# Second block: the gates' added row in one TensorE pass over 128 rows, and the convolution's columns turned inside the first gate

## The reference, cut to what matters

```python
h = rmsnorm_2(x, g_mix[l])
proj = jnp.einsum('bsd,dc->bsc', h, w_in[l])
q_a, k_a, v_a, q_i, k_i, w_i, conv_in, q_m, gate_logits = jnp.split(proj, split_points, axis=-1)
...
o_a = dsa_attention(q_a, k_a, v_a, q_i, k_i, w_i, topk)
o_b = conformer_conv(conv_in, conv_w[l], conv_b[l], ln_g[l], ln_b[l])   # u = a * sigmoid(gte), then 31 taps
o_m = memory_attention(q_m, mem, g_mem[l], w_mem_kv[l], g_qm[l], g_km[l])
gates = jax.nn.sigmoid((gate_logits + b_gate[l]).astype(jnp.float32)).astype(x.dtype)
gates = gates.reshape(B, S, N_BRANCHES, D)
merged = (gates[:, :, 0] * (o_a @ w_br_a[l]) + gates[:, :, 1] * (o_b @ w_br_b[l])
          + gates[:, :, 2] * (o_m @ w_br_m[l]))
```

## Time and profile before

| what | value |
|---|---|
| device time, three runs | 1715.82, 1716.11, 1717.97 us; median 1716.11 us |
| the profiled execution: its own time | 1714.42 us |
| its span, first to last instruction | 1712.6 us |
| TensorE / VectorE / ScalarE busy | 96% / 71% / 51% of the span |
| mean granted TensorE clock | 0.976 |
| L1786, the added row: matmul records | 24, at 587 ns in the median and up to 1214 ns |
| where they lie | 1123.3 to 1249 us of the span |

### The profile page before, as it was taken

One profiled execution on the slowest core, in us unless ns is written; L12 is line 12 of the kernel. 1 busy time (PEld: TensorE's weight loads), 2 busy tenths in 40 slices (PEclk: granted clock), 3 DMA queues, 4 the chain that ended last, 5 costly groups with the idle time before them and its releaser, 6 DMA issues.

```text
span 1712.6 us, 19789 instructions
## 1 busy us (share of the span) xinstructions
PE 1640.2 (96%) x7803; PEld 1299.2 (76%) x7803; DVE 1221.9 (71%) x1721; ACT 869.3 (51%) x1244; POOL 55.4 (3%) x87
## 2 busy tenths in 40 slices
PE   6999999999999999999999999999989999999998
PEld 2888877888868887668788888766768888787776
DVE  3989987989876855535655555685487578888986
ACT  3545454444454444355544444544355357776874
POOL 1010100000000000000000001000010000000000
PEclk9999999999999999999999999998599999999999
DMA  9998857988868754422655544442033338998993
GB/s 349 375 348 294 315 164 249 321 285 299 287 222 267 247 187 161 162 98 85 230 181 192 190 137 127 157 154 95 25 101 92 99 139 315 349 317 306 347 336 127
DMA packets 199603, 373.77 MB, mean 218 GB/s; under 512 B 8928, under 2 KB 102550, under 8 KB 199504
## 3 DMA queue, kind: packets, MB, share of 16 engines
q1 hardware_dynamic: 184080, 316.28, 54.2%
q0 software_dynamic: 15024, 55.07, 9.2%
q10 hardware_dynamic: 400, 1.10, 0.2%
HBM read 371.37 MB, written 1.05 MB: 217 GB/s over the span
## 4 chain that ended last, share of the span: by engine, by line
PE 86%; DVE 7%; ACT 5%; issue 1%; DMA 1%; SPq 0%; DVEq 0%; ACTq 0%
PE banks L520 23%; PE banks L522 23%; PE banks L521 23%; PE banks L747 2%; PE banks L1298 2%; PE banks L1325 1%; ACT full L719 1%; PE banks L1777 1%; DVE ul L464 1%; PE banks L672 1%; PE banks L889 1%; ACT uh L453 1%; PE banks L2249 1%; PE banks L2294 1%; PE banks L1312 1%; PE banks L1786 1%
## 5 line engine op out<-in xcount | busy, mean ns | idle before, releaser
L464 DVE TENSOR_TENSOR ul<-raw,uh 128x1024 fp32r<-128x1024 f32 (+2 forms) x548 | 659.2, 1210 | 216.9 <-ACT uh L453 208.3
L453 ACT ACTIVATE uh<-raw 128x1024 fp32r<-128x1024 f32 (+2 forms) x548 | 571.3, 1050 | 466.3 <-PE banks L522 457.6
L520 PE MATMUL banks<-uh,hh 128*128 128x512 f32 (+2 forms) x1280 | 522.2, 408 | 8.4 <-DVE hl L784 5.4
L522 PE MATMUL banks<-uh,hl 128*128 128x512 f32 (+2 forms) x1280 | 499.9, 391 | 0.0
L521 PE MATMUL banks<-ul,hh 128*128 128x512 f32 (+2 forms) x1280 | 499.0, 390 | 0.0
L520 PEld LDWEIGHTS banks<-uh,hh 128*128 128x128 f32 x1280 | 243.5, 190 | 72.5 <-issue 12.7
L521 PEld LDWEIGHTS banks<-ul,hh 128*128 128x128 f32 x1280 | 243.7, 190 | 53.1 <-issue 7.7
L522 PEld LDWEIGHTS banks<-uh,hl 128*128 128x128 f32 x1280 | 243.2, 190 | 50.6
L520 PE MATMUL banks<-uh,bh 128*128 128x512 f32 x528 | 209.8, 397 | 9.4 <-DVE bl L943 4.2
L522 PE MATMUL banks<-uh,bl 128*128 128x512 f32 x528 | 205.9, 390 | 0.0
L521 PE MATMUL banks<-ul,bh 128*128 128x512 f32 x528 | 205.6, 389 | 0.0
(11 more groups left out here) (311 smaller groups left out, 1400.3 us busy)
## 6 DMA issues: line engine op xcount, KB each, us to landing
raw<-in_ffn_w_in SPq DMA_DIRECT2D x176, 512.0 KB, 5.3
raw<-in_w_up SPq DMA_DIRECT2D x64, 1024.0 KB, 5.6
arena<-in_ada_w POOLq DMA_DIRECT2D x46, 1024.0 KB, 7.8
raw<-in_ffn_w_out SPq DMA_DIRECT2D x44, 1024.0 KB, 6.9
raw<-in_w_down SPq DMA_DIRECT2D x32, 1024.0 KB, 5.3
raw<-in_ada_w SPq DMA_DIRECT2D x26, 1024.0 KB, 6.7
raw<-in_w_in SPq DMA_DIRECT2D x22, 1024.0 KB, 5.0
raw<-in_w_mem_kv SPq DMA_DIRECT2D x4, 1024.0 KB, 5.9
```

The costliest lines, as they stand in the source:

```text
L453: act.e.activation(uh[r][:, 0:w], raw[m % NRAW][:, h * w:(h + 1) * w], AF.Copy).then_inc(act_done, ta.put("hi", u))
L464: dve.e.tensor_tensor(ul[r][:, 0:w], raw[m % NRAW][:, h * w:(h + 1) * w], uh[r][:, 0:w].bitcast(F32), ALU.subtract).then_inc(dve_done, tv. ...
L520: pe.e.matmul(o, a, wh, start=s0, stop=False)
L522: mm = pe.e.matmul(o, b, wh, start=False, stop=s1)
```

## The change

1. A new tile `gb` of 128 rows x 520 fp32r columns. Columns 0 to 511 hold the high parts of the six added rows in rows 0 to 5, their low parts in rows 32 to 37, and zeros elsewhere. Columns 512 to 517 hold the selection: column j has a one in rows j and 32 + j. `gate_rows_dve` fills it with five VectorE instructions and stands in VectorE's program between the norm's parts and the projections; it waits for both loads of `b_gate`.
2. `b_gate` is loaded twice on POOL's queue, to `adab[0:6]` and `adab[32:38]`.
3. A gate's added row is one fp32r matmul over all 128 rows for each bank (`gsel` x `gbias`), in place of the float32 one over 6 rows. It waits for `gate_rows_dve` in place of the load.
4. `conv_turn`, with its two counterparts on ScalarE and VectorE, moves from the middle of projection 3 to the middle of gate (0,0).
5. To make room, the second probability buffer is `adab`, and the arena, `cc` and `st` shrink.

```diff
@@ memory
-ARENA = 11332
+ARENA = 10816
-        cc = sb("cc", [P, 48])
+        cc = sb("cc", [P, 46])
-        st = sb("st", [P, 280])
+        st = sb("st", [P, 278])
+        gb = sb("gb", [P, 520], F32R)
-        pr6 = [wide_bufs[2], A(512)]
+        pr6 = [wide_bufs[2], adab[:, :]]
@@ gates
+        gsel, gbias = gb[:, 512:518], gb[:, 0:512]
+
+        def gate_rows_dve(dve):
+            low = gb[32:38, 0:512]
+            dve.wait_ge(loaded("b_gate"), 32)
+            dve.e.memset(gb[:, 0:518].bitcast(F32), 0.0).then_inc(dve_done, tv.put())
+            dve.own()
+            dve.e.tensor_tensor(gsel[0:38, :], ident[0:38, 0:6], ident[0:38, 32:38], ALU.add).then_inc(
+                dve_done, tv.put())
+            dve.e.tensor_copy(gbias[0:6, :], adab[0:6, :]).then_inc(dve_done, tv.put())
+            dve.e.tensor_copy(low, adab[32:38, :]).then_inc(dve_done, tv.put())
+            dve.own()
+            dve.e.tensor_tensor(gbias[32:38, :], adab[32:38, :], low.bitcast(F32), ALU.subtract).then_inc(
+                dve_done, tv.put("gb"))
+
-        def gates_pe(pe, g, c):
+        def gates_pe(pe, g, c, mid=None):
             j = 2 * g + c
-            pe.wait_ge(loaded("b_gate"), 16)
+            pe.wait_ge(dve_done, tv("gb"))
             for b in PAIRS[0]:
                 pe.take(b)
-                pe.e.matmul(PB[b], ident[0:6, j:j + 1].to_broadcast([6, P]), adab[0:6, :], start=True, stop=False)
-            linear(pe, ("gt",), KD, lh, ll, parts_ready(pe, "mix"), [[b] for b in PAIRS[0]], first=False,
+                pe.e.matmul(PB[b], gsel[:, j:j + 1].to_broadcast([P, P]), gbias, start=True, stop=False)
+            linear(pe, ("gt",), KD, lh, ll, parts_ready(pe, "mix"), [[b] for b in PAIRS[0]], first=False, mid=mid,
                    done=("gate", g, c))
...
@@ the three programs (TensorE's shown; ScalarE's and VectorE's likewise)
                 linear(pe, ("pj",), KD, lh, ll, parts_ready(pe, "mix"), [[b] for b in banks],
-                       mid=conv_turn if n == 3 else None, done=("pj", n))
+                       done=("pj", n))
...
-                    gates_pe(pe, g, c)
+                    gates_pe(pe, g, c, conv_turn if (g, c) == (0, 0) else None)
...
             scaled_dve(dve, "mix", KD, hh, hl, lambda k: col("g_mix_2", k), lambda k: 0.0)
+            gate_rows_dve(dve)
             dve.e.memset(uT[:, :, 0:30], 0.0).then_inc(dve_done, tv.put("u0"))
@@ POOL's loads
-            load("b_gate", adab[0:6, :], I["b_gate_2"].rearrange("a (j n) -> (a j) n", n=512))
+            for r in (0, 32):
+                load("b_gate", adab[r:r + 6, :], I["b_gate_2"].rearrange("a (j n) -> (a j) n", n=512))
```

More of the change, by code:

```diff
@@ L1790, in gates_pe, with gates_act @@
                 pe.frees(b, act_done, ta, "gate", g, c, t)
-        def gates_act(act, g, c):
-            units_act(act, ("gt",), KD)
+        def gates_act(act, g, c, mid=None):
+            units_act(act, ("gt",), KD, mid=mid)
             act.wait_ge(pe_done, tp("gate", g, c))
@@ L1908, in mix_act @@
             for n in range(len(PROJ)):
-                units_act(act, ("pj",), KD, mid=conv_turned if n == 3 else None)
+                units_act(act, ("pj",), KD)
                 act.wait_ge(pe_done, tp("pj", n))
@@ L1941, in mix_act @@
                 for c in range(2):
-                    gates_act(act, g, c)
+                    gates_act(act, g, c, conv_turned if (g, c) == (0, 0) else None)
             act.later.flush("qa")
@@ L1986, in mix_dve @@
             for n in range(len(PROJ)):
-                units_dve(dve, ("pj",), KD, mid=conv_weights if n == 3 else None)
+                units_dve(dve, ("pj",), KD)
                 if n == 1:
@@ L2002, in mix_dve @@
                     dve.later.add(heads_dve(dve, QA, lambda: taps_dve(dve, taps, 2)), "qa")
-            for _ in range(4):
-                units_dve(dve, ("gt",), KD)
+            for n in range(4):
+                units_dve(dve, ("gt",), KD, mid=conv_weights if n == 0 else None)
             dve.later.flush("qa")
```

## The result

The changed kernel's median was 1698.63 us in four runs (1697.13 to 1702.14) against 1715.96 for the kernel before; the ratio is 0.9899, with a 95% interval of 0.9881 to 0.9918. That is 17.3 us, where 13.6 were forecast; 1702.5 was predicted, 1698.5 to 1709 was the range. Single runs of both kernels scatter. I take 16.3 us as the gain to be explained; its 95% interval from these runs is 14.6 to 18.0.

What follows compares the result with a forecast made beforehand. TensorE, busy 96% of the span, was taken to bound the kernel. Row 9.65 plus clock 4.6 minus slower rise 0.7 gave 13.6 us, so 1716.11 became 1702.5 us; range 1698.5 to 1709.

Steps and rivals of the forecast that it cites:

- The added row: At six gate starts, one fp32r matmul per bank replaces the float32 one over 6 rows: 9.65 us gained.
- the 2.8 us set aside for it: Possible cost at the gates' added rows if a broadcast fp32r column's weight load took twice the matmul's 0.23 us, unhidden.
- The clock: After gates (2,0) and (2,1), both clock falls disappear as the light stretch ahead of the linear shortens: 4.6 us gained.
- larger gain: Whole kernel: more gained than forecast if the executions behind the median lose more falls than the profiled one; chance 0.03.
- The rise at gate (1,0): Behind the heads' flush, 0 to 2.7 us more at half speed before the clock rises: loss taken as 0.7 us.
- The turn: 1.38 us of TensorE work turning the columns moves from projection 3 to gate (0,0): net zero.
- Gate rows and second load: Ahead of the projections, five VectorE instructions (2.3 us, under 6.8 us of cover) and one more load: cost 0.
- VectorE late next: At the first head, VectorE's rotation of q would end 1.2 us ahead of TensorE's need: barely enough.
- Rival 1: In the gates, the clock falls stay, since only idle TensorE gaps cause them: 1707.1 us; chance 0.16.
- rival 3: At the added row, fp32r over a broadcast column runs like float32; no gain, falls stay: 1716.1 us; chance 0.05.
- rival 2: At the heads and keys' norm, VectorE's chain can't come earlier and takes TensorE's place: about 1710.6 us; chance 0.08.
- rival 4: Slower: clock falls at five gate starts and at the turn, 3.0 us each, 18 in all: 1720.5 us; chance 0.03.

Runs made afterwards that it cites:

- e5: Changed kernel, but the row is one plain float32 matmul per bank over all 128 rows, 122 of them zeros; 1708.72 us, ratio 0.9941 to the kernel before.
- e7: Changed kernel, but each bank gets four fp32r matmuls over all 128 rows in place of one; 1711.38 us, ratio 0.9958 to the kernel before.
- e6: Changed kernel, but each bank gets four fp32r matmuls over 6 rows in place of one over 128; 1716.02 us, ratio 0.9998 to the kernel before.
- e2: Kernel before with only the turn moved into gate (0,0), float32 row over 6 rows kept; 1717.18 us, ratio 0.9999 to the kernel before.
- e8: Changed kernel unaltered, measured again beside the kernel before in five rounds; 1701.61 us, ratio 0.9903.
- e11: Changed kernel unaltered, measured again as partner of other variants; 1700.67 us, ratio 0.9905 to the kernel before.
- e1: Changed kernel, but the turn of the columns stays in projection 3; median 1700.81 us, ratio 0.9905 to the kernel before.
- e3: Changed kernel, but gates (0,0), (2,0) and (1,1) use the other pair of banks; 1697.06 us, ratio 0.9886 to the kernel before.

## Why the prediction was right, and where its sizes were off

- **The added row, 9.65 us.** Its working has two errors that nearly cancel in the profile. The linear's first matmul comes 0.30 us later than I put it, since I left the second bank's weight load of 0.18 out of the sum. But before, the linear's first matmul took 0.43 us behind the row, at full clock, and now it takes 0.24 (L521 at 1138.09). Counted to the second matmul, gate (0,1) went from 2.41 us (1137.08 to 1139.49, by the earlier trace rows and that 0.43) to 1.23: 1.18 gained, forecast 1.27. Gate (1,0) gained 3.1, from 1229.66 to the second full matmul at 1234.09 before, against 1221.31 to 1222.59 now; 2.84 was forecast. Over many runs the row's time is worth somewhat less: the changed kernel against e5 gives 7.1 us in the means (about 2.3 to 11.9), and with the 1.2 of the first full matmuls, which e5 doesn't pay any more, 8.3. The weight load of a broadcast fp32r column, which I had no row for, takes 0.185 us in the median, and the 2.8 us set aside for it did not come.
- **The clock, 4.6 us.** The cause was right, rows at work, and e5 to e7 show it. The Trainium skill (TensorE: Matmul & The Clock Gate, "HAM oscillation") names only gaps in which TensorE is idle; here e6 lost the clock with TensorE as busy as in e7. The size was the term that failed: I took the falls of one execution for the kernel's, 1.6 + 2.7 + 0.3. The kernel before against e5 gives 9.2 us in the mean, 8.0 without the first full matmuls. The profile of e2, whose row is that of the kernel before, has four falls in the gates instead of two (its clock is below 1.00 in all three stretches shown above) and a span of 1719.9 us; the profiled one of before was among the quickest of its kind. This is the "larger gain" to which I gave 0.03. The prediction counted the idle 0.65 us ahead of the row into the light work, too; it stands unchanged in the changed kernel (0.69), without a fall, and whether it matters beside a row over 6 rows no run shows.
- **The rise at gate (1,0), loss 0.7.** The sign was wrong, by the very mechanism of the term before it: a row over 128 rows lets the clock rise earlier. The full matmuls began at 1222.17, and one cost 0.24 at 1223.87, 1.7 us later, against 3.2 before, some 0.7 us gained. Counted from the row's start the rise comes after 2.5 us here, 3.5 in e8 and 3.6 in e11, against 6.6 and 8.5 for the float32 row over 6 rows. This gain is part of the 8.0.
- **The turn, zero.** Shown by e1 and e2. VectorE's copy ran at 1134.14 with no wait ahead of it, and ScalarE's in its idle time.
- **Gate rows and second load, zero.** 2.2 us under a cover of 6.8.
- **VectorE late next, 1.2 us to spare.** 1.1 in the trace, and e3 used it up.
- **Sum.** 8.3 + 8.0 = 16.3 measured by parts, row and clock; 9.65 + 3.9 = 13.6 forecast. The split is known to some 5 us only, the sum to 1.7. The row came out smaller and the clock larger, and part of the forecast's nearness is that they offset; the first median of 1698.63 stood 0.1 us inside the range, the mean of 15 runs 2 us below the forecast. Rival 1 (falls stay) and rival 3 (no single pass) are refuted, rival 2 held only for a kernel quicker still, and rival 4's falls at the turn and the gate starts did not come.

## What to carry to other kernels

A matmul over few rows is dear twice: it holds TensorE as long as one over all rows, and the clock may fall behind it, or rise later, which costs the full matmuls that follow. Pad it to all rows with zeros, and make it fp32r with a low part if float32's four-fold time is on the path. Before counting what a fall of the clock costs, look at many executions: one trace shows one draw.

## What the runs showed that I had not expected

- The first full matmul behind a 6-row one costs 0.43 us at full clock, in the kernel before and in e6, whatever the type; behind a 128-row one it costs 0.23, in e5 and e7. The chain at gate (0,0), first of e6, then of e7:

```profile
1124.46 2.12 PE banks L1804 x8
1126.58 0.43 PE banks L521
...
1127.23 0.23 PE banks L523
...
1127.68 0.28 PE banks L522
1127.97 0.43 PE banks L523
```

```profile
1124.87 2.12 PE banks L1804 x8
1126.99 0.23 PE banks L521
1127.22 0.23 PE banks L522
```

  In e6 the clock also falls 3.2 us behind the row's start (0.43 from 1127.97 on), in the very gate that had no fall in the trace of the kernel before (e2 has one there too). In e6 the full matmul's weights are loaded only at 1126.50, as the row's last matmul ends.
- Float32 over 128 rows, with no change of type at all, gave 9.2 of the 16.3 us in the means, about half of the gain.
- Falls come elsewhere too, in some executions only: e8's profile has 0.53 from 1372 to 1375.4, in the second block's routing, where the first profile of the same kernel has 1.00. They go with the scatter of 2.9 us: of the changed kernel's 15 runs, the three with a mean clock of 0.982 took 1696.3 to 1697.6 us, and the four with 0.977 took 1703.3 to 1705.1. That is why differences of 2 us stayed open here.
- From the heads' flush to the rise at gate (1,0) the clock is 0.50 for 44 to 48 us in the three traces with a row over 6 rows and for 37 to 41 in the other eleven. The row only moved the end of that stretch; its long part, the flush itself, no variant touched.
